# One triangular form on TensorE and its turn on VectorE: the recurrent scan and the expert blocks of a two-block model

## What is computed

```python
def _rwkv7_scan(s0, r, w, k, v, a, b):              # 8 heads of 64, both directions
    def step(S, inp):
        r_t, w_t, k_t, v_t, a_t, b_t = inp
        sa = jnp.einsum('bhvk,bhk->bhv', S, a_t)
        S = S * w_t[:, :, None, :] + sa[..., None] * b_t[:, :, None, :] + v_t[..., None] * k_t[:, :, None, :]
        return S, jnp.einsum('bhvk,bhk->bhv', S, r_t)
...
def _moe_swiglu(h, router_w, router_b, w1, w3, w2): # 8 experts, 1024 -> 2816 -> 1024, top 2
    ...
    for e in range(N_EXPERTS):
        out = out + gates[..., e:e + 1] * _swiglu(h, w1[e], w3[e], w2[e])
```

## Time and profile before

| | us |
|---|---|
| median of 3 runs (3294.92 to 3304.92) | 3294.95 |
| the profiled execution | 3293.41 |
| its span | 3291.6 |
| TensorE busy | 3116.3 (95%) |
| VectorE busy | 1283.0 (39%) |
| ScalarE busy | 588.3 (18%) |

### The profile page before, as it was taken

The page is one execution under the profiler, slowest core; times in us unless marked ns, Lnnn a source line. Parts: engine busy times, 40 slices in busy tenths (PEclk is TensorE's granted clock), DMA queues, the critical chain, the costliest instruction groups (busy, mean ns, idle before and its releaser), DMA issues.

```text
span 3291.6 us, 52527 instructions
## 1 busy us (share of the span) xinstructions
PE 3116.3 (95%) x22488; PEld 2069.7 (63%) x22488; DVE 1283.0 (39%) x2836; ACT 588.3 (18%) x1314; POOL 0.2 (0%) x4
## 2 busy tenths in 40 slices
PE   7999899999999999999999999999999879988998
PEld 5454799997344443457745555445557568876887
DVE  1568666666799887503410101000112232122211
ACT  2114222222211111203310110010111220012000
POOL 0000000000000000000000000000000000000000
PEclk8999999999999999999999999999999889999999
DMA  7241001001577886330189999999984114531452
GB/s 264 75 154 51 1 1 40 1 1 39 189 239 243 245 248 187 123 99 25 70 317 362 357 339 337 343 362 367 349 231 130 51 52 141 153 115 51 133 148 64
DMA packets 351595, 551.15 MB, mean 167 GB/s; under 512 B 14512, under 2 KB 292400, under 8 KB 348048
## 3 DMA queue, kind: packets, MB, share of 16 engines
q1 hardware_dynamic: 351376, 547.89, 50.2%
HBM read 546.80 MB, written 1.05 MB: 166 GB/s over the span
## 4 chain that ended last, share of the span: by engine, by line
PE 89%; DVE 6%; ACT 2%; DMA 2%; issue 1%; SPq 0%; DVEq 0%; ACTq 0%
PE bank L666 15%; PE bank L1337 14%; PE bank L928 9%; PE bank L1130 8%; PE bank L1359 8%; PE bank L1517 7%; PE bank L1144 3%; PE bank L631 3%; PE bank L745 3%; PE bank L1171 2%; PE bank L1075 2%; DVE mix L2079 2%; PE bank L912 1%; PE bank L1282 1%; DMA arena<-in_ada_w 1%; PE bank L1426 1%
## 5 line engine op out<-in xcount | busy, mean ns | idle before, releaser
L666 PE MATMUL bank<-a,ring 128*128 128x256 f32 (+1 forms) x1792 | 454.8, 417 | 19.0 <-ACT a L1614 12.0
L666 PEld LDWEIGHTS bank<-a,ring 128*128 128x128 f32 x1792 | 344.9, 193 | 126.5 <-issue 74.5
L2079 DVE SCALAR_TENSOR_TENSOR mix<-arena,csil,mix 128x256 f32<-128x256 f32 x1008 | 402.0, 476 | 45.6 <-ACT mix L1618 45.6
L1337 PE MATMUL bank<-ring,arena 128*32 128x352 f32 x5376 | 406.9, 461 | 2.7 <-ACT small L1876 2.7
L1337 PEld LDWEIGHTS bank<-ring,arena 128*32 128x32 f32 x5376 | 175.1, 110 | 221.4 <-issue 220.4
L1130 PE MATMUL bank<-a,ring 128*128 128x512 f32 x704 | 307.5, 596 | 6.8 <-ACT a L1614 6.8
L1130 PEld LDWEIGHTS bank<-a,ring 128*128 128x128 f32 x704 | 133.2, 191 | 179.7 <-issue 178.0
L1517 PE MATMUL bank<-arena,ring 128*128 128x256 f32 x1024 | 223.5, 379 | 1.9 <-DVE arena L2736 1.9
L1618 ACT ACTIVATE arena<-bank 128x256 f32<-128x256 f32 (+1 forms) x303 | 142.0, 473 | 451.7 <-PE bank L928 199.2
L2638 DVE TENSOR_TENSOR arena<-arena,bank 128x352 f32<-128x352 f32 x48 | 25.0, 521 | 501.3 <-ACT arena L1889 501.3
L1359 PE MATMUL bank<-ring,arena 128*32 128x256 f32 (+1 forms) x3840 | 219.0, 380 | 0.6 <-issue 0.6
(11 more groups left out here) (411 smaller groups left out, 3360.6 us busy)
## 6 DMA issues: line engine op xcount, KB each, us to landing
ring<-in_moe_w SPq DMA_DIRECT2D x224, 704.0 KB, 8.4
ring<-in_mlp_w SPq DMA_DIRECT2D x64, 1024.0 KB, 5.5
ring<-in_moe_w SPq DMA_DIRECT2D x112, 512.0 KB, 8.4
arena<-in_ada_w SPq DMA_DIRECT2D x96, 512.0 KB, 3.8
arena<-in_w_ada SPq DMA_DIRECT2D x48, 512.0 KB, 3.6
ring<-in_ffn_w SPq DMA_DIRECT2D x22, 1024.0 KB, 8.5
arena<-in_moe_w SPq DMA_DIRECT2D x32, 704.0 KB, 8.8
ring<-in_moe_w SPq DMA_DIRECT2D x48, 384.0 KB, 8.4
```

What stands on the lines that cost most here:

```text
L666: i = mm(bank[b][:, 0:n], ws[:, k, t * P:t * P + P], rhs[:, k, sl], start=(k == 0), stop=(k == KT - 1))
L1337: i = mm(b[32 * t:32 * t + 32, 0:PART], ac_[:, k, 32 * g:32 * g + 32], ws[i_][:, PART * t:PART * t + PART], start=(k == 0), stop=(k == KT ...
L2079: ins = V.scalar_tensor_tensor(dst, x, cond, dst, ALU.mult, ALU.add)
```

## The change

In the scan, TensorE computes one form of E2, E4, T2, T4, T8 and of the first merge, and VectorE makes the other from it with a transpose, which turns each 32x32 block (at these steps the matrices are zero outside such blocks). The second merge still computes both forms, the third the one that is used. `first_tt` goes. VectorE's other operations of the unit stand in another order, and `decays` no longer waits on TensorE for VectorE; ScalarE waits instead, for the state of unit u - 2, before it overwrites `ex`.

In the experts' blocks, `gather` gives tokens by 32 partitions, and VectorE turns them from the bank into `ac_`; VectorE turns `hid` into `gT`, and TensorE's turns and ScalarE's copies of both go. As 32x32 turns leave the four column parts on four groups of 32 partitions, a load has to bring rows in that order too: four groups of 32 rows, a quarter of the matrix apart. The down product has 22 pieces of 128 rows for 24. In the second block's attention, `scores2` is issued one unit earlier.

The diff, cut (lines without a sign are as before):

```diff
-PIECES = ((0, 128), (128, 128), (256, 96))
-BLOCKS_AT = [(p, t, i) for p in range(2) for t in range(4) for i in range(3)]
-ITEMS = 32 + len(BLOCKS_AT)
+DOWN = [(p, c) for p in range(2) for c in range(PART // 32)]
+ITEMS = 32 + len(DOWN)
...
-                                src = w["moe_w3" if i % 2 else "moe_w1"][0]
-                                src = src[one, k * P:k * P + P, n0:n0 + MCOLS]
+                                src = w["moe_w3" if i % 2 else "moe_w1"][0][one, :, n0:n0 + MCOLS]
+                                src = src.rearrange("e (t r) n -> (e t) r n", t=4)[:, 32 * k:32 * k + 32, :]
                             else:
-                                p, t, piece = BLOCKS_AT[i - 32]
-                                o, n = PIECES[piece]
-                                f0 = MCOLS * p + PART * t + o
-                                src = w["moe_w2"][0][one, f0:f0 + n, :]
-                                dst = dst[0:n, 0:D]
-                            src = src.rearrange("e p n -> p (e n)")
+                                p, c = DOWN[i - 32]
+                                src = w["moe_w2"][0][one, MCOLS * p:MCOLS * p + MCOLS, :]
+                                src = src.rearrange("e (t r) n -> (e t) r n", t=4)[:, 32 * c:32 * c + 32, :]
+                                dst = dst[:, 0:D]
                             sy.dma_start(dst, src).then_inc(m_full[i % MRING], 16)
...
             def decays(u):
-                if u >= 2:
-                    pe.wait_ge(vec_done, at(VE, ("state", u - 2)))
-                elif u == 0:
+                if u == 0:
...
-            def squared(name, u, p, i, both=True):
+            def squared(name, u, p, i):
+                two(POWER_BANK[p], 0, half_of(ED, i, p, 1), half_of(ED, i, p, 0)
+                    ).then_inc(pe_done, did(PE, (name, u, p)))
+
+            def grown(name, u, p, by, i, halves=(0,)):
+                t_ = half_of(TD, i, p, 0)
+                for half in halves:
+                    ins = two(GROW_BANK[p], 256 * half, *((t_, by) if half else (by, t_)))
...
+                grown(("Tm", lv), u, p, z, 1 - lv % 2, ((0,), (0, 1), (1,))[lv])
...
                     grown("T2", u, p, half_of(ED, 1, p, 0), 0)
+                    pe.wait_ge(vec_done, at(VE, ("E2 turned", u, p)))
                     squared("E4", u, p, 1)
...
             def gather():
-                for f in range(KT):
+                for g in range(GROUPS_OF):
                     for c in range(2):
-                        i = mm(bank[0 if f >= 4 else 4][:, (f % 4) * CAP:(f % 4) * CAP + CAP],
-                               atok[:, c, f * P:f * P + P], pm[:, c, :], start=(c == 0), stop=(c == 1),
+                        for q in range(4):
+                            i = mm(bank[4 * (g // 2)][32 * q:32 * q + 32, 256 * (g % 2):256 * (g % 2) + 256],
+                                   pm[:, c, 32 * g:32 * g + 32], atok[:, c, 256 * q:256 * q + 256],
...
-                        if p == 1 and k in (2, 3, 4):
...
-                            hidden_turned(0, k - 2)
...
             scores2(0)
+            scores2(1)
             for w_ in range(len(DIFF_UNITS)):
-                if w_ + 1 < len(DIFF_UNITS):
-                    scores2(w_ + 1)
+                if w_ + 2 < len(DIFF_UNITS):
+                    scores2(w_ + 2)
...
             def decays(u):
+                if u >= 2:
+                    ac.wait_ge(vec_done, at(VE, ("state 1", u - 2)))
...
-            def first_tt(u):
...
+            def power_turned(name, u, p, i):
+                ve.wait_ge(act_done, at(AC, (name, u, p)))
+                V.transpose(ED[i][:, p, 256:512], ED[i][:, p, 0:256]
+                            ).then_inc(vec_done, did(VE, (name + " turned", u, p)))
...
+            def inverse_turned(name, u, p, i, before):
+                ve.wait_ge(vec_done, before)
+                V.transpose(TD[i][:, p, 256:512], TD[i][:, p, 0:256]).then_inc(vec_done, did(VE, name))
...
+            def gathered(g, inc, counter, name):
+                V.transpose(ac_[:, g, :], bank[4 * (g // 2)][:, 256 * (g % 2):256 * (g % 2) + 256]
+                            ).then_inc(inc, did(counter, (name, g)))
...
+                def hidden_turned(p, g):
+                    ve.wait_ge(ve_moe, e * per + at(VEM, ("hid", p, g)))
+                    V.transpose(gT[:, p, g, :], hid[:, p, g, :]).then_inc(ve_moe, did(VEM, ("gT", p, g)))
```

More of the change, by code:

```diff
@@ L978, in _ @@
                     decays(u + 1)
[L979 removed]
+                pe.wait_ge(vec_done, at(VE, ("T1", u)))
                 for p in range(2):
@@ L1756, in _ @@
                 power_out("E4", u, 0)
-                power_out("E8", u, 1, both=False)
+                power_out("E8", u, 1)
                 if not last:
@@ L1863, in _ @@
             pper, vper = at(PEM, ("per", "moe")), at(VEM, ("per", "moe"))
-            def gathered(name, inc, counter):
-                for h in range(2):
-                    act(ac_[:, 4 * h:4 * h + 4, :], cut(bank[4 - 4 * h], 0, 4, CAP), ACT.Copy
-                        ).then_inc(inc, did(counter, name if h else (name, 0)))
-            ac.wait_ge(pe_done, at(PE, "gather first"))
-            gathered("gathered first", act_done, AC)
             ac.wait_ge(act_done, now(AC))
@@ L1899, in _ @@
                 act(pgt[:, 2, :], bank[2][:, 0:256], ACT.Copy).then_inc(ac_moe, did(ACM, "gates"))
-                of_pe("gather")
-                gathered("gathered", ac_moe, ACM)
-                of_pe(("down", len(BLOCKS_AT) - 1))
+                of_pe(("down", len(DOWN) - 1))
                 for g in range(GROUPS_OF):
@@ L2372, in bridge_mask @@
                 V.tensor_tensor(bm[lv], dm[u % 2], off, ALU.mult).then_inc(vec_done, did(VE, ("bm", u, lv)))
-            for part in range(3):
+            for part in range(5):
                 decayed(0, part)
@@ L2381, in _ @@
             diagonal(0, 1)
-            first_tt(0)
+            for p in range(2):
+                power_turned("E2", 0, p, 1)
+            for lv in range(3):
+                bridge_mask(0, lv)
             for u, (d, c, pg) in enumerate(UNITS):
                 last = u + 1 == len(UNITS)
-                for p in range(2):
-                    grown("T2", u, p, 0, at(VE, ("TT1", u)))
-                    if not last:
-                        decayed(u + 1, p)
-                for p in range(2):
-                    grown("T4", u, p, 1, at(VE, ("T2", u, p)))
-                    if not last and p == 0:
-                        decayed(u + 1, 2)
-                bridge_mask(u, 0)
+                grown("T2", u, 0, 0, at(VE, ("T1", u)))
+                if not last:
+                    decayed(u + 1, 0)
+                power_turned("E4", u, 0, 0)
+                if not last:
+                    decayed(u + 1, 1)
+                grown("T2", u, 1, 0, at(VE, ("T1", u)))
+                power_turned("E4", u, 1, 0)
+                grown("T4", u, 0, 1, at(VE, ("T2", u, 0)))
+                if not last:
+                    decayed(u + 1, 2)
+                grown("T4", u, 1, 1, at(VE, ("T2", u, 1)))
                 for p in range(2):
                     grown("T8", u, p, 0, at(VE, ("T4", u, p)))
-                bridge_mask(u, 1)
-                bridge_mask(u, 2)
+                    if not last and p == 0:
+                        decayed(u + 1, 3)
+                    inverse_turned(("T8 turned", u, p), u, p, 1, at(VE, ("T8", u, p)))
+                if not last:
+                    decayed(u + 1, 4)
                 if not last:
@@ L2413, in _ @@
                     diagonal(u + 1, 1)
-                    first_tt(u + 1)
+                    bridge_mask(u + 1, 0)
+                    for p in range(2):
+                        power_turned("E2", u + 1, p, 1)
                 ve.wait_ge(pe_done, at(PE, ("s", u)))
@@ L2427, in _ @@
                                     ).then_inc(vec_done, did(VE, ("state", u)))
+                if not last:
+                    bridge_mask(u + 1, 1)
+                    bridge_mask(u + 1, 2)
                 ve.wait_ge(vec_done, now(VE))
@@ L2604, in _ @@
             pper, aper = at(PEM, ("per", "moe")), at(ACM, ("per", "moe"))
+            def gathered(g, inc, counter, name):
+                V.transpose(ac_[:, g, :], bank[4 * (g // 2)][:, 256 * (g % 2):256 * (g % 2) + 256]
+                            ).then_inc(inc, did(counter, (name, g)))
             ve.wait_ge(pe_done, at(PE, "gather first"))
+            for g in range(GROUPS_OF):
+                gathered(g, vec_done, VE, "gathered first")
+            ve.wait_ge(vec_done, now(VE))
             counts.count[VEM] = per
@@ L2643, in _ @@
                     back_added(f, ve_moe, VEM, "h")
+                of_pe("gather")
+                for g in range(GROUPS_OF):
+                    gathered(g, ve_moe, VEM, "gathered")
                 ve.wait_ge(ve_moe, e * per + now(VEM))
```

109 lines of the change are left out of this document (42 added, 67 removed).

## The result

The changed kernel takes **4991.83 us** (4986.53 to 4996.13), the kernel before 3294.93 us in the same comparison: a ratio of 1.514, 95% interval 1.511 to 1.517. The forecast was 5240 us with a range of 4950 to 5880.

A forecast was written before the change was run, and what follows sets the result against it. TensorE, busy 95%, was taken to bound the kernel. With expert loads on four engines, the stream from 1550.5 plus 2854 ends at 4404.5; plus 9, 827 and 1.8 gives 5242, said as 5240 us, range 4950 to 5877.

The forecast's parts named there:

- What decides: Experts' transfers: a load of four row groups is dealt to four engines, 97 GB/s, 2854 us of stream; chance 0.80.
- The rate of an engine: Experts' transfers: one engine moves 24.3 GB/s, the middle of 22.0 and 26.5; four give 97 GB/s.
- 17% to spare: Experts' stage before the change: transfers hidden, at 83% of what 16 engines show, with 17% to spare.
- The tail: After the last expert load: a piece, the outputs' copies and the last products back, 9 us.
- The attention: Second block's attention: scores issued two units ahead leave the chain where VectorE waited, 5 us saved, between 0 and 10.
- The scan: 24 of 76 products leave each unit: 5.1 us saved a unit, some 80 us over 16 units, bounds 56 and 97.
- rival (C): VectorE bounds the scan, with turns at 0.69 us or more; the scan gives 56 us or less; no chance given.
- The stall of 1 us in a unit: Scan, unit border: TensorE waits for T2 for about 1 us, with 24 fewer products to cover VectorE's operations.
- The experts on TensorE: Fewer down pieces, no turns, cheaper gather: 6.6 us of 99.4 saved a block, 53 us over eight, hidden under transfers.
- What would show it: Signs: experts' stage some 2850 us, share near 0.25, about 97 GB/s, half clock, slow landings; scan units of 23.4 us.
- (A): Experts' transfers keep 16 engines and the stage stays TensorE's: 3155 us, 3110 to 3200; chance 0.12.
- (B): Experts' transfers: four engines get in each other's way, pairs at half rate, 49 GB/s, 8100 us in all; chance 0.07.

The follow-up runs named there:

- e4: The kernel before with only the source of its 128-row expert loads taken as 4 groups of 32 rows, 96-row loads plain: 4963.84 us.
- e6: The changed kernel with the source of each expert load taken as 8 groups of 16 rows instead of 4 of 32: 3724.25 us.
- e9: The changed kernel with the source's two row dimensions swapped, 32 rows outermost and the 4 groups inside, same rows per load: 3121.65 us.
- e5: The changed kernel with the source of each expert load taken as 16 groups of 8 rows instead of 4 of 32: 3391.31 us.
- e1: The changed kernel with expert loads of 128 rows in a row again, the row order made on chip by reading columns in runs of 32: 3128.89 us.
- e3: The kernel before with only the last attention's scores issued two units ahead: 3270.91 us, ratio 0.991.
- e7: The changed kernel with each expert load issued as four loads of 32 rows in a row, same rows to the same places: 3515.39 us.
- e10: e1 with each expert load issued as four loads of 32 rows, all in a row in memory: 3521.96 us.
- e12: e5 with the groups 9 rows apart in memory instead of 64 (88 in the down weights): 3388.74 us.
- e11: e10 with each load writing every fourth partition instead of 32 neighbouring ones: 3594.09 us.

## Why the prediction was right, and where its steps were off

**What decides** was right in kind. The share of 0.26, e4 with the shape alone, e6 with twice the groups and e9 with the order swapped all show four engines because of four groups. The Trainium skill's rule (*DMA: Bandwidth & Descriptors*, section *Why a DMA increments its semaphore by 16 and not by 1*), the largest number up to 16 that divides the slowest dimension of both sides, gives 4, 8, 16 and 16 for the changed kernel, e6, e5 and e9, and the shares agree: 0.26, 0.51, 1.02, 0.97. It says nothing that would tell e5 from e9.

**The rate of an engine** was the term that was mis-sized. I took 24.3 GB/s, the middle between 22.0 and 26.5. It is 26.5, the upper bound, which was the row of engines always at work. The 22.0 was no limit of an engine. It is a mean over a stretch of the kernel before in which 16 engines fall to 240 to 295 GB/s for 40 us (1900 to 1940) at a share of 1.0, and four engines never do. In that stretch the down weights come in, some in loads of 96 rows. e1 loads the same bytes by 128 rows, and wherever its share is at 1.00 or above between 1700 and 1960 (stretches of 10 us) it moves 384 to 418 GB/s. So the 96-row loads are the suspect; no run changes them alone. The same mean misled me on the spare: a share of 1.01 at 352 GB/s is a row of engines without idle time, so "17% to spare" did not follow from it. From issue to landing the stream takes 4173.3 - 1549.7 = 2624 us, not 2854. With the start 0.8 us earlier, its end is 231 us before the predicted one. With the 19 us by which the attention was put too low, that is the whole difference between the sum of 5242 and 4992. The mechanism was right, and the measured time stands at the low end of the range, 15 us above its bound of 4977, because that bound was worked out with the 26.5.

**The tail** behind the last load: 9 us predicted, 4182.8 - 4173.3 = 9.5 measured.

**The attention** was put at 5 us, between 0 and 10, and is 24 (27 in e3 by itself). The step failed in what it counted. The 20.2 us of idle TensorE stood in the row I quoted, as did the clock of 0.80; I took the scores to leave only part of a wait. With scores two ahead nearly the whole wait goes, and the products run at full clock on top.

**The scan** was right in size: 80 us predicted, 82 by the records of L928. The unit is 467.54 - 444.43 = 23.1 us for 23.4, VectorE is busy 21.51 to 22.34 us of 28, 78%. Three lines of VectorE there (mean ns), for the rows that stood in for them:

```profile
L2329 DVE TENSOR_TENSOR arena<-ring,bank 128x256 f32<-128x256 f32 x14 | 5.7, 407 | 3.7 <-PE bank L928 3.6
...
L2322 DVE STREAM_TRANSPOSE arena<-arena 128x256 f32<-128x256 f32 x12 | 5.3, 440 | 2.0 <-ACT arena L1602 2.0
...
L2335 DVE STREAM_TRANSPOSE ring<-ring 128x256 f32<-128x256 f32 x8 | 3.6, 446 | 0.3
```

A turn is 0.44 us, for the 0.42 that I took and the 0.69 that rival (C) needed, so (C) did not come. The stall of 1 us in a unit is there, but not where I put it. The chain at a unit's border:

```profile
444.86 0.46 PE bank L928 x4
445.42 0.42 DVE arena L2329
445.84 0.34 DVE ring L2275
446.18 0.14 issue
446.32 2.00 PE bank L912 x16
```

TensorE does not wait for T2. It waits before the grams of the next unit (L912) for the receptance factor (L2275). The change put that operation behind the first addition of T8 (L2329) in VectorE's order. The same price came from another queue position, which I had not followed.

**The experts on TensorE**: 6.6 us a block predicted, 99.4 - 91.8 = 7.6 in e1, where it can be seen. In the changed kernel it is hidden, as predicted.

**What would show it** came, with the stream at 106 GB/s in place of about 97 and three exceptions. The clock stood at 0.65 to 0.74 in the quoted and neighbouring stretches, not at half for most of the stage: TensorE works for some 45% of the time, in bursts, and both levels occur.

```profile
2010.00:2015.00 5.00, 0.00 (x0) 0.00 (x0) 0.00 (x0) 0.00 (x0) 0.00 (x0) 1.00 0.25 106
...
2030.00:2035.00 5.00, 3.53 (x25) 1.42 (x29) 0.00 (x0) 0.00 (x0) 0.00 (x0) 0.50 0.27 110
```

A load did not take many tens of us to land, since SyncE was held at its issue and the queue stayed short; the last landed in 22.8 us. And the wait for T2, above.

**The rivals.** (A), 16 engines kept, gave 3155 us; e1 is that case made true, at 3129, and by the corrected terms 3293 - 82 - 61 - 24 = 3126. (B), pairs of engines on a common way, is refuted: four engines reach 26.5 GB/s each, as much as each of 16 at their best. The Trainium skill's rule on ports 32 partitions apart (*SBUF — State Buffer*, section *Door 1: The DMA port swizzle*) thus cost nothing that can be seen with four engines at work. Whether it has a part in the slow packets of 16 engines (e5, e7, e10) no run here shows.

## What to carry to other kernels

Before a load is reshaped, look at its outermost dimension on both sides: when it shrinks from 128 to 4 rows, 12 of 16 engines stand idle, and the sign of it in a profile is a flat share of 0.26 with a rate as flat. If the chip needs rows in another order, put the long dimension outermost (e9; its rows land on other partitions, so the products that read them have to follow, and e9 itself computes with other weights), or read in another order where it is free, as in runs of 32 columns by TensorE (e1), which made this change worth 5% instead of costing 51%. A good part of a change can be hidden under its bad part: here 169 us of gain (3297.6 - 3128.9).

## What was not expected of the hardware

- An issue on SyncE gets longer when its engines are behind, in the median: 6.3 us with 4 engines, 2.9 with 8, 0.54 with 16 at full rate (e9). A long issue was a symptom here, not a cause.
- 16 busy engines can be slow: a share of 1.02 at 276 to 299 GB/s (e5, e12) and of 1.03 at 235 (e7, e10), against 415. A share near 1.0 does not mean that the rate is at its best. Each packet of a row takes 335 to 407 ns there, 215 at the best rate. The cause is open.
- A source with two row dimensions costs 0.54 us to issue, against 0.33 (e9, e1); one that writes every fourth partition 0.47 against 0.32 (e11, e10).
